# Norm sums of a two-block transformer kernel: pairs added on GpSimd, one unit back at full width, other banks, second block begun with k, q and v

## The chip, the cores and the metric

The kernel runs on one core of a Trainium2 chip. The metric is the device time of one execution in microseconds (us). The time of before is the median of three runs. Engines are named as in the profile: PE is TensorE (PEld its weight load), DVE VectorE, ACT ScalarE, POOL GpSimd, SP SyncE, which issues the DMAs of the weights.

## The reference, cut to what matters

Two transformer blocks over 512 tokens with 1024 features, all in fp32. The first holds two layers (Fox attention, then differential attention), each with a convolutional feed-forward net:

```python
def first_block(x, ...):
    for layer in range(DEPTH):                       # 2
        h = _fox_attention(...) or _diff_attention(...)
        x = _layer_norm(DN_ALPHA * x + h, ln_attn_g[layer], ln_attn_b[layer])
        f = _conv_ffn(x, ...)
        x = _layer_norm(DN_ALPHA * x + f, ln_ffn_g[layer], ln_ffn_b[layer])

def rms_norm(x, g):
    xf = x.astype(jnp.float32)
    xf = xf * lax.rsqrt(jnp.mean(xf * xf, axis=-1, keepdims=True) + EPS)
    return (xf * g.astype(jnp.float32)).astype(x.dtype)
```

The second block takes an RMS norm of that result and makes one projection out of it: keys, values and queries of a grouped-query attention with 8 query and 2 key heads, and the x, z, B, C and time-step inputs of a state-space scan (SSD) with a convolution over time. Both branches are mixed, projected, normed, added to x, and followed by a norm, a gated feed-forward net and a last norm. The change touches the eight norms. Four are layer norms, which need the mean of the values and of the squares; four are RMS norms, which need the mean of the squares alone.

## The kernel before, in words

**Data.** Activations lie feature-major: 8 blocks of 128 features by 512 tokens. Products are made to fp32 precision out of two parts of each operand: XH is the rounded activation, XL what is left of it, HI and LO the same of a weight. A weight *unit* is a slab of up to 1024 features by 256 outputs; SP loads it into RAW, ACT rounds it to HI (L1766, four instructions of 128x512), and LO = RAW - HI is made by DVE for the even quarters and by POOL for the odd ones (L2646). Each k-step of a tile is then three matmuls, HI with XH, HI with XL, LO with XH (L1441).

**Order.** `agenda()` writes one list of steps, and every engine follows that list in order, each taking the steps in which it has a part. Where work runs beside other work (attention beside the projections), `alongside()` mixes the two at a rate out of `RATES`, and `SLOW` sets how often the turning of the second block's queries gets a step. `LATE` and `STATS` hold the steps of a norm back by so many tiles.

**Halves.** A norm needs all 1024 features of a token before it can begin. `ending()` therefore runs the last units before a norm in two halves of 256 tokens: first all of their tiles for tokens 0 to 255, then for 256 to 511, with twice as many matmuls of half the width. `beginning()` does the same with the first units behind the norm, so that half 0 of the next projection can run while half 1 is normed.

**The norms.** They are called a0, f0, a1, f1 (layer norms behind attention and net of the two layers), c0 (the second block's first norm), m, p and f (RMS norms; m and p stand together, as f1 and c0 do, through `two_norms()`). YH is the residual sum that a norm works on. A1 sums its values, A2 its squares. A full-width tile (step `acc`) is squared on ACT into S and added on POOL into A2 (L2666), and its values into A1 (L2668). A tile pair of a half (step `acch`) is squared into a buffer P (L1789) and not added. The step `st0` sums over the 128 partitions on PE by matmuls with one output column each (128x1): over A2 and A1, then over every YH block and every P that was not added. For c0 and p the square of each pair (`sqp`, L1795) is followed by a step `stq` with its four one-column matmuls. Each matmul that the program orders stands in the trace as two records, so `x8` in a row of the trace is four ordered matmuls. After `st0` come `st1`, `stb` and the four pairs of `lnp` (T, XH on ACT, XL on POOL).

**Banks.** PSUM has eight banks. The norms use 6 for one half and 5 for the other; c0 and p the other way round.

**Ends of units around the change.** The attention output is four units, `ao` in layer 0 and `bo` in layer 1. Unit 0 runs at full width, 1 to 3 in halves. Units 0 and 1 of the net (`up0`, `up1`) then begin in halves. The second block begins with `ck` (keys) and `cq` 0 and 1 (queries) in halves, then `cv` (values and time steps, 160 columns) at full width, then six units `cx` whose tiles go through the convolution (cxe, cx1, cxt). The step `cacs` needs a chain on ACT with three table loads and on DVE, which starts from the last tile of `cv`.

Of the kernel before, what the change touches and what calls it, by code (L numbers as in the profile page):

```python
# [110 lines left out]
def const_arrays():  # L111
# [32 lines left out]
RATES = (0.37, 0.18, 1.15, 0.36, 1.0, 0.9, 0.9)  # L144
AHEAD = 5
SLOW = 2
# [21 lines left out]
    "acch": (("sq", 1),),  # L168
    "sqp": (("sq", 1),),
    "stq": (("ssum", 1),),  # L170
# [70 lines left out]
class Agenda:  # L241


    def __init__(self):
        self.steps, self.tiles, self.order, self.bank_of, self.free_of = [], [], [], {}, {}
        self.unit_end, self.count = {}, {}
        self.slot_of, self.slot_free = {}, {}
# [18 lines left out]
def raised(step, tiles):  # L266
# [15 lines left out]
    if k == "acc":  # L282
        _, n, j, mean = step
        adds = (1 if j == 0 else 2) if mean else (1 if j else 0)
# [24 lines left out]
def unit_sequence():  # L309
# [9 lines left out]
    out += [("ck", 0), ("cq", 0), ("cq", 1), ("cv", 0)] + [("cx", i) for i in range(6)] + [("cz", i) for i in range(4)]  # L319
# [7 lines left out]
def agenda():  # L327
# [8 lines left out]
    slots = {"S": [None] * 2, "T": [None] * 3, "P": [None] * 3}  # L336
# [16 lines left out]
    def at_slot(step, pool, q, release):  # L353

        if q is None:
            q = taken_slots[pool] % len(slots[pool])
            taken_slots[pool] += 1
        ag.slot_of[step], ag.slot_free[step] = q, slots[pool][q]
        slots[pool][q] = (release[0], release[1])
# [134 lines left out]
    def ending(n, groups, src, banks, evict, chain):  # L494
# [12 lines left out]
        for f in range(2):  # L507
            for (p, keys), bank in zip(groups, banks[f]):
# [23 lines left out]
                put("acch", n, p, f)  # L532
                at_slot(steps[-1], "P", p - 1, ("ssum", ("st0", n, f)))
# [4 lines left out]
    def beginning(units, last=False):  # L538
# [8 lines left out]
        for f in range(2):  # L547
            for q, (kind, key, widths, banks, evac) in enumerate(units):
# [13 lines left out]
                t0, rows = ts[q]  # L562
                if kind == "mm":
# [47 lines left out]
    def accumulate(n, j, mean):  # L611
        s = put("acc", n, j, mean)
        if j:
            at_slot(s, "S", None, ("ac", s))

    def chain(n, f, mean, each, begun=False):

        if not begun:
            for _ in range(LATE):
                yield  # L620
            while bank_of_norm(n, f) in norm_at:
                yield
            norm_at.add(bank_of_norm(n, f))
            s = put("st0", n, f)
            at_bank(s, bank_of_norm(n, f))
# [10 lines left out]
    def bank_of_norm(n, f):  # L636
        return 6 - (f if n not in ("c0", "p") else 1 - f)

    def normed(n, kind):
        def each(f, p):  # L640
            s = put(kind, n, f, p)
            at_slot(s, "T", None, ("xl", s))
# [6 lines left out]
    def layer_norm(n):  # L649
        return lambda f: chain(n, f, True, normed(n, "lnp"))  # L650

    def two_norms(n, n2):

        def each(f, p):
            if n == "f1":
                s = put("lnr", n, f, p)
                at_slot(s, "T", None, ("la", s))
            else:
                s = put("n1", n, f, p)
            s2 = put("sqp", n2, f, p)  # L660
            at_slot(s2, "S", None, ("ssum", ("stq", n2, f, p)))
# [2186 lines left out]
```

## Time and profile before

| | |
|---|---|
| median of 3 runs | 2492.13 us (2486.79 to 2497.16) |
| profiled execution: time, span | 2489.54 us, 2487.8 us |
| PE busy | 2332.1 us, 94% of the span |
| DVE, ACT, POOL busy | 1101.3, 1014.5, 917.1 us (44%, 41%, 37%) |
| granted TensorE clock, mean | 0.948 |

Busy time of PE is its matmul time; a granted clock of 0.5 is 1.2 GHz and 1.0 is 2.4 GHz, and a mean in between says how the stretch was shared. The chain of work that ended last runs over PE for 84% of the span, so what counts are PE's own instructions, its waits and its clock.

### The profile page before, as it was taken

Reading aid. Unit: us, or ns where it says so; the run is one execution under the profiler, and the core shown is the slowest. Engines: PE = TensorE matmul, PEld = TensorE weight load, DVE = VectorE, ACT = ScalarE, POOL = GpSimd, SP = SyncE. Lnnn points to the kernel's source line nnn. Section 1 sums busy time; section 2 is a strip of 40 time slices with the busy share of each in tenths; the row PEclk is TensorE's granted clock in tenths of the full one; section 3 lists DMA queues with packets and bytes.
Section 4 is the critical chain, followed back from the end, with each engine's and each line's share of the span. In section 5 each row is a group of like instructions: output and inputs, shape, how many; then the busy total and the mean of one; then the engine's idle time right before and its main releaser. Section 6 shows DMA issues by size and latency. Waiting matters only on the chain.

```text
span 2487.8 us, 31338 instructions
## 1 busy us (share of the span) xinstructions
PE 2332.1 (94%) x12565; PEld 1972.8 (79%) x12576; DVE 1101.3 (44%) x1826; ACT 1014.5 (41%) x2061; POOL 917.1 (37%) x718
## 2 busy tenths in 40 slices
PE   7999999999998887999999988998899999999998
PEld 6788898888887776988888887665487888888887
DVE  3545454554335664454543332545644333333322
ACT  5656354443255553344442243443244333333222
POOL 3655343344456642243344232002432332222232
PEclk9999999999999898899999886996899999999999
DMA  3111122222223210122223111000012221222221
GB/s 149 58 60 52 35 102 102 89 98 94 77 94 94 68 56 31 52 102 102 91 92 104 53 49 39 35 35 17 1 43 77 102 102 52 87 100 102 88 103 64
DMA packets 30880, 183.27 MB, mean 74 GB/s; under 512 B 3984, under 2 KB 6160, under 8 KB 12944
## 3 DMA queue, kind: packets, MB, share of 16 engines
q1 hardware_dynamic: 30736, 181.27, 20.7%
q8 instruction: 100, 1.64, 0.3%
q14 instruction: 44, 0.36, 0.0%
HBM read 174.97 MB, written 2.10 MB: 71 GB/s over the span
## 4 chain that ended last, share of the span: by engine, by line
PE 84%; DVE 5%; ACT 4%; POOL 3%; issue 2%; DMA 0%; another core or an unknown queue 0%; SPq 0%; POOLq 0%; ACTq 0%; DVEq 0%
PE PS L1441 82%; POOL LO L2646 1%; PE PS L1568 1%; PE PS L1678 1%; POOL XL L2646 1%; DVE aQS L2153 0%; ACT bP L1993 0%; DVE LO L2153 0%; ACT HI L1766 0%; DVE bQS L2153 0%; PE PS L1616 0%; POOL A_f L2666 0%; ACT bQS L1979 0%; ACT T_a L1815 0%
## 5 line engine op out<-in xcount | busy, mean ns | idle before, releaser
L2646 POOL TENSOR_TENSOR LO<-RAW,HI 128x512 fp32r<-128x512 f32 (+1 forms) x382 | 542.2, 1436 | 648.8 <-ACT HI L1766 648.6
L1441 PE MATMUL PS<-XH,HI 128*128 128x512 f32 (+2 forms) x1752 | 675.2, 385 | 40.1 <-POOL XL L2646 20.1
L1441 PE MATMUL PS<-XL,HI 128*128 128x512 f32 (+2 forms) x1752 | 657.0, 375 | 0.0
L1441 PE MATMUL PS<-XH,LO 128*128 128x512 f32 (+2 forms) x1752 | 656.7, 375 | 0.0
L1441 PEld LDWEIGHTS PS<-XH,HI 128*128 128x128 f32 (+1 forms) x1752 | 337.7, 193 | 117.4 <-issue 39.4
L2153 DVE TENSOR_TENSOR LO<-RAW,HI 128x512 fp32r<-128x512 f32 (+3 forms) x286 | 314.2, 1109 | 218.9 <-ACT HI L1766 218.9
L1766 ACT ACTIVATE HI<-RAW 128x512 fp32r<-128x512 f32 (+3 forms) x668 | 365.9, 607 | 97.4 <-DMA RAW<-wall 96.9
L1441 PEld LDWEIGHTS PS<-XH,LO 128*128 128x128 f32 (+1 forms) x1752 | 337.6, 193 | 58.5 <-issue 1.1
L1441 PEld LDWEIGHTS PS<-XL,HI 128*128 128x128 f32 (+1 forms) x1752 | 338.3, 193 | 51.8 <-issue 1.0
L1441 PE MATMUL PS<-HH,HI 128*128 128x512 f32 (+1 forms) x660 | 235.7, 357 | 3.3 <-POOL LO L2646 3.2
L1441 PE MATMUL PS<-HL,HI 128*128 128x512 f32 (+1 forms) x660 | 231.9, 351 | 0.0
L1441 PE MATMUL PS<-HH,LO 128*128 128x512 f32 (+1 forms) x660 | 231.8, 351 | 0.0
L1441 PEld LDWEIGHTS PS<-HH,HI 128*128 128x128 f32 x660 | 128.2, 194 | 21.0 <-POOL LO L2646 3.6
L1441 PEld LDWEIGHTS PS<-HL,HI 128*128 128x128 f32 x660 | 128.2, 194 | 16.9 <-issue 1.4
L1441 PEld LDWEIGHTS PS<-HH,LO 128*128 128x128 f32 x660 | 128.2, 194 | 15.4
L1441 PE MATMUL PS<-HI,XH 128*128 128x256 f32 (+1 forms) x416 | 129.4, 311 | 8.3 <-DVE aVL L2153 2.8
L2678 POOL TENSOR_TENSOR UT<-UT 128x512 f32<-128x512 f32 x44 | 56.4, 1283 | 206.2 <-ACT UT L1844 206.2
L1441 PE MATMUL PS<-LO,XH 128*128 128x256 f32 (+1 forms) x416 | 123.3, 296 | 0.0
L1441 PE MATMUL PS<-HI,XL 128*128 128x256 f32 (+1 forms) x416 | 123.3, 296 | 0.0
L1842 ACT ACTIVATE UT<-PS,SM 128x512 f32<-128x512 f32 x88 | 67.5, 771 | 126.4 <-PE PS L1441 126.4
L2251 DVE SCALAR_TENSOR_TENSOR UT<-PS,SM,UT 128x511 f32<-128x511 f32 x88 | 65.4, 744 | 93.1 <-ACT UT L1842 93.1
L2684 POOL TENSOR_SCALAR aP<-aP,aRC 128x128 f32<-128x128 f32 (+1 forms) x64 | 69.4, 1086 | 91.9 <-DVE aRC L2332 91.7
(345 smaller groups left out, 3596.0 us busy)
## 6 DMA issues: line engine op xcount, KB each, us to landing
RAW<-wall SPq DMA_DIRECT2D x138, 1024.0 KB, 4.8
RAW<-wall SPq DMA_DIRECT2D x24, 896.0 KB, 4.6
bROT<-bTQ SPq DMA_DIRECT2D x64, 64.0 KB, 2.0
RAW<-wall SPq DMA_DIRECT2D x5, 512.0 KB, 3.5
XF<-xT SPq DMA_DIRECT2D x4, 512.0 KB, 5.7
outT<-XR SPq DMA_DIRECT2D x8, 256.0 KB, 2.3
FP<-cfp SPq DMA_DIRECT2D x1, 1024.0 KB, 6.8
MKF<-cmask SPq DMA_DIRECT2D x1, 704.0 KB, 11.0
```

The lines of the kernel that those rows point to most:

```text
L1441: return e.matmul(out, a, b, start=start, stop=stop)
L1568: m = e.transpose(PS[bank][:, 128 * kb:128 * kb + 128], aP[:, 512 * (n % 4) + 128 * kb:512 * (n % 4) + 128 * kb + 128], IDN)
L1678: m = e.transpose(PS[bank][:, 128 * kb:128 * kb + 128], p[:, 128 * kb:128 * kb + 128], IDN)
L1766: act(HI[i % 3][:, c], RAW[i % 3][:, c], ACT.Copy).then_inc(SEM["hi"], 1)
L1842: act(x, PS[ag.tiles[t].bank][:, :], ACT.Identity, bias=col(f"cb{lay}", f), scale=col(f"cw{lay}2", f)).then_inc(SEM["ui"], 1)
L2153: return e.tensor_tensor(out, x, h.bitcast(F32), ALU.subtract)
L2251: e.scalar_tensor_tensor(out=x[:, 1:512], in0=ps[:, 0:511], scalar=col(f"cw{lay}1", f), in1=x[:, 1:512], op0=ALU.mult, op1=ALU.add).then_i ...
L2646: return e.tensor_tensor(out, x, h.bitcast(F32), ALU.subtract)
L2678: e.tensor_tensor(g, g, v, ALU.mult).then_inc(SEM["um"], 1)
L2684: e.tensor_scalar(p, p, aRC[:, n:n + 1], None, ALU.mult).then_inc(SEM["dg"], 1)
```

## The change

- **Sums by pairs.** A2 and A1 become 1024 wide: two tiles side by side. The squares of tiles 0 and 1 are written straight into A2, and POOL copies the values of both into A1. Every later full-width tile is added by POOL to its side, and so are now the pairs 1 and 2 of the halves (in m, and in c0 and p the pairs 1 and 2 of `sqp`). Pair 3 is still summed by PE. Buffers P and the step `stq` go; `st0` is one step for all norms.
- **Units split.** `attn_out` runs unit 1 of `ao` and `bo` at full width; halves are left for 2 and 3.
- **Banks.** Half 0 of a norm uses bank 6, half 1 bank 4 (f1, m) or 5; c0 and p use 5 and 6. The first units of the net change their banks with it.
- **Second block.** The order becomes ck, cq0, cv, cq1, of which ck, cq0 and cv begin in halves. `SLOW`, two of the `RATES`, and `LATE` for c0 and p are changed.

```diff
-RATES = (0.37, 0.18, 1.15, 0.36, 1.0, 0.9, 0.9)
+RATES = (0.37, 0.18, 1.25, 0.36, 1.6, 0.9, 0.9)
-SLOW = 2
+SLOW = 1
...
-    out += [("ck", 0), ("cq", 0), ("cq", 1), ("cv", 0)] + [("cx", i) for i in range(6)] + [("cz", i) for i in range(4)]
+    out += [("ck", 0), ("cq", 0), ("cv", 0), ("cq", 1)] + [("cx", i) for i in range(6)] + [("cz", i) for i in range(4)]
...
+    def squares(step, n, f, to_sum, add):
+
+        if add or to_sum:
+            at_slot(step, "S", ("ac", step) if add else ("ssum", ("st0", n, f)))
+        if dict(raised(step, tiles)).get("ac"):
+            add_before[step] = added.get(n)
+            added[n] = step
...
-                put("acch", n, p, f)
-                at_slot(steps[-1], "P", p - 1, ("ssum", ("st0", n, f)))
+                squares(put("acch", n, p, f), n, f, p == 3, p < 3)
...
+        for _ in range(2 if n in ("c0", "p") else LATE):
+            yield
...
     def bank_of_norm(n, f):
-        return 6 - (f if n not in ("c0", "p") else 1 - f)
+        if n in ("c0", "p"):
+            return 5 + f
+        return 6 if f == 0 else 4 if n in ("f1", "m") else 5
...
-            s2 = put("sqp", n2, f, p)
-            at_slot(s2, "S", None, ("ssum", ("stq", n2, f, p)))
-            yield
-            yield
-            s2 = put("stq", n2, f, p)
+            squares(put("sqp", n2, p, f), n2, f, p == 3, p in (1, 2))
+            yield
+            yield
...
-        ending(n, [(i, [(name, i)]) for i in (1, 2, 3)], src, [[2, 3, 4], [7, 0, 1]], residual_half(n), layer_norm(n))
+        for j, t in enumerate(lin_fm((name, 1), src)):
+            residual(n, 2 + j, t)
+        ending(n, [(i, [(name, i)]) for i in (2, 3)], src, [[4, 7], [0, 1]], residual_half(n), layer_norm(n))
...
         beginning([("mm", ("ck", 0), (128,), [0], qk_evac(4)), ("mm", ("cq", 0), (128, 128), [1, 2], qk_evac(0)),
-                   ("mm", ("cq", 1), (128, 128), [3, 4], qk_evac(2))], last=True)
-
-        def evac(c, t):
-            return ("cdt", put("cvev", c, t))
-        lin_tm(("cv", 0), "X", evac)
+                   ("mt", ("cv", 0), None, [3, 7], lambda c, t: ("cdt", put("cvev", c, t)))], last=True)
         converted[0] = True
+        for j, t in enumerate(lin_fm(("cq", 1), "X")):
+            qk_evac(2)(j, t)
...
+            elif kind in ("acch", "sqp") and step in ag.add_before:
+                n, p, f = a
...
+                e.wait_ge(*when("sq", *step))
+                if ag.add_before[step] is not None:
+                    e.wait_ge(*when("ac", *ag.add_before[step]))
+                s2, s1 = half_sums(nb["A2"], f), half_sums(nb["A1"], f)
+                e.tensor_tensor(s2, s2, by2(buf(n, "S", step)[:, :]), ALU.add).then_inc(SEM["ac"], 1)
+                if n in MEANED:
+                    e.tensor_tensor(s1, s1, pair(YH, p, f), ALU.add).then_inc(SEM["ac"], 1)
```

PE's order where a0's statistics of half 0 are made (`st0`, in the middle of the last units of `ao`; A_a_143 is A2, A_a_142 is A1, P_a are the squares of pairs that are not added), of before:

```order
L1441 MATMUL PS<-NEGC,FP 128x4
L1441 MATMUL PS<-FP,A_a_143 128x1
L1441 MATMUL PS<-FP,A_a_142 128x1
L1441 MATMUL PS<-FP,A_a_143 128x1
L1441 MATMUL PS<-FP,A_a_142 128x1
L1441 MATMUL PS<-FP,YH 128x1 x4
L1441 MATMUL PS<-FP,P_a_150 128x1 x4
L1441 MATMUL PS<-FP,YH 128x1 x4
L1441 MATMUL PS<-FP,P_a_151 128x1 x4
L1441 MATMUL PS<-FP,YH 128x1 x4
L1441 MATMUL PS<-FP,P_a_149 128x1 x4
```

The same place of the changed kernel:

```order
L1447 MATMUL PS<-NEGC,FP 128x4
L1447 MATMUL PS<-FP,A_a_143 128x1
L1447 MATMUL PS<-FP,A_a_142 128x1
L1447 MATMUL PS<-FP,A_a_143 128x1
L1447 MATMUL PS<-FP,A_a_142 128x1
L1447 MATMUL PS<-FP,A_a_143 128x1
L1447 MATMUL PS<-FP,A_a_142 128x1
L1447 MATMUL PS<-FP,A_a_143 128x1
L1447 MATMUL PS<-FP,A_a_142 128x1
L1447 MATMUL PS<-FP,YH 128x1 x4
L1447 MATMUL PS<-FP,S_a_145 128x1 x4
```

28 ordered one-column matmuls became 16; the 128x4 one ahead of them stays.

POOL's order from the first tile of `ao` to the odd quarters of LO_61, the first unit of the net (LO_59 and LO_60 are those of the last two `ao` units; XL is the norm's own), of before:

```order
L2661 COPY A_a_142<-YH 128x512
L2666 TENSOR_TENSOR A_a_143<-A_a_143,S_a_144 128x512
L2668 TENSOR_TENSOR A_a_142<-A_a_142,YH 128x512
L2646 TENSOR_TENSOR LO_59<-RAW_56,HI_62 128x512 x2
L2646 TENSOR_TENSOR LO_60<-RAW_57,HI_63 128x512 x2
L2646 TENSOR_TENSOR XL<-T_a_146,XH 128x2x256
L2646 TENSOR_TENSOR XL<-T_a_147,XH 128x2x256
L2646 TENSOR_TENSOR XL<-T_a_148,XH 128x2x256
L2646 TENSOR_TENSOR XL<-T_a_146,XH 128x2x256
L2646 TENSOR_TENSOR LO_61<-RAW_58,HI_64 128x512 x2
```

And of the changed kernel, up to the first XL:

```order
L2640 TENSOR_TENSOR LO_59<-RAW_56,HI_62 128x512 x2
L2661 TENSOR_TENSOR A_a_143<-A_a_143,S_a_144 128x512
L2663 TENSOR_TENSOR A_a_142<-A_a_142,YH 128x512
L2661 TENSOR_TENSOR A_a_143<-A_a_143,S_a_145 128x512
L2663 TENSOR_TENSOR A_a_142<-A_a_142,YH 128x512
L2640 TENSOR_TENSOR LO_60<-RAW_57,HI_63 128x512
L2671 TENSOR_TENSOR A_a_143<-A_a_143,S_a_144 128x2x256
L2673 TENSOR_TENSOR A_a_142<-A_a_142,YH 128x2x256
L2640 TENSOR_TENSOR LO_60<-RAW_57,HI_63 128x512
L2671 TENSOR_TENSOR A_a_143<-A_a_143,S_a_144 128x2x256
L2673 TENSOR_TENSOR A_a_142<-A_a_142,YH 128x2x256
L2640 TENSOR_TENSOR XL<-T_a_146,XH 128x2x256
```

Six more additions stand there, and LO_60, the last `ao` unit's, lies between them, the second odd quarter behind the additions of half 0's pair 2.

ACT's order at the end of `ao`, where the squares of the last pairs and the rounding of the net's first weights (HI_64) lie, of before:

```order
L1819 ACTIVATE XH<-T_a_146 128x2x256
L1789 ACTIVATE P_a_151<-YH 128x512
L1766 ACTIVATE HI_64<-RAW_58 128x512 x4
L1789 ACTIVATE P_a_149<-YH 128x512
L1766 ACTIVATE HI_62<-RAW_56 128x512 x2
```

And of the changed kernel:

```order
L1813 ACTIVATE XH<-T_a_146 128x2x256
L1789 ACTIVATE S_a_145<-YH 128x512
L1762 ACTIVATE HI_64<-RAW_58 128x512 x4
L1762 ACTIVATE HI_62<-RAW_56 128x512 x2
```

In the changed kernel the square ahead of HI_64 is that of the last pair (3) of half 1, and no longer that of pair 2.

## Rows read from the trace of the kernel before

A line of a timeline gives the start in us, the duration in us from first to last instruction of the group, the engine, the line of the kernel, and how many records it holds; in brackets stands the idle time before it and what ended it.

**Rows 1.** The page: busy time of each engine.

```profile
PE 2332.1 (94%) x12565; PEld 1972.8 (79%) x12576; DVE 1101.3 (44%) x1826; ACT 1014.5 (41%) x2061; POOL 917.1 (37%) x718
```

**Rows 2.** Busy time by stretch: us, engines' busy (count), granted clock, DMA share, GB/s.

```profile
983.00:1062.00 79.00, 76.06 (x575) 74.85 (x576) 35.16 (x51) 30.13 (x58) 28.81 (x21) 0.91 0.15 54
1376.00:1476.00 100.00, 85.46 (x574) 83.33 (x573) 35.08 (x61) 32.95 (x65) 29.07 (x22) 0.81 0.12 41
1476.00:1552.00 76.00, 65.67 (x381) 57.85 (x381) 22.11 (x43) 31.41 (x59) 21.58 (x17) 0.73 0.17 58
1701.00:1726.00 25.00, 19.43 (x75) 13.86 (x74) 12.87 (x20) 10.03 (x19) 5.13 (x3) 0.51 0.01 5
2044.00:2120.00 76.00, 70.42 (x561) 69.38 (x560) 27.38 (x46) 28.75 (x53) 21.13 (x15) 0.96 0.16 56
```

**Rows 3.** Waits of PE over the whole span: us, times, longest.

```profile
PE PS L1441 <- ACT S_m L1795: 2.1, 3, 0.8
...
PE PS L1441 <- ACT cPT L2071: 1.6, 2, 0.8
```

**Rows 4.** Waits of PE from 1405 to 1552 us: us, times, longest.

```profile
PE PS L1441 <- POOL XL L2646: 9.4, 4, 3.3
PE PS L1441 <- DVE cADT L2496: 6.1, 1, 6.1
PE PS L1441 <- ACT S_f L1795: 3.5, 2, 1.7
PE PS L1441 <- ACT FP L2076: 2.6, 1, 2.6
PE PS L1441 <- DVE LO L2153: 1.6, 1, 1.6
```

**Rows 5.** Timeline of PE, a0's statistics of half 0: start, us, work.

```profile
292.06 0.28 PE L1441 MATMUL PS<-aOH,LO 128*128 128x256 f32 x1
292.18 0.28 PE L1441 MATMUL PS<-NEGC,FP 128*128 128x4 f32 x2
292.31 1.03 PE L1441 MATMUL PS<-FP,A_a 128*128 128x1 f32 x8
293.21 1.03 PE L1441 MATMUL PS<-FP,YH 128*128 128x1 f32 x8
...
301.53 0.56 PE L1441 MATMUL PS<-aOH,HI 128*128 128x256 f32 x1
```

**Rows 6.** Busy time by stretch around both halves' statistics of a0.

```profile
291.00:302.00 11.00, 11.00 (x72) 11.00 (x71) 0.26 (x2) 1.36 (x2) 0.00 (x0) 0.70 0.01 1
302.00:306.00 4.00, 4.00 (x22) 4.00 (x22) 0.64 (x4) 0.30 (x1) 0.00 (x0) 0.55 0.01 2
320.00:330.00 10.00, 10.00 (x75) 10.00 (x73) 1.94 (x4) 1.76 (x4) 1.82 (x2) 0.80 0.21 87
330.00:334.00 4.00, 4.00 (x24) 4.00 (x24) 1.18 (x4) 1.86 (x4) 1.28 (x1) 0.64 0.00 0
```

**Rows 7.** Timeline of POOL in the last units of ao.

```profile
272.69 1.30 POOL L2666 TENSOR_TENSOR A_a<-A_a,S_a 128x512 f32<-128x512 f32 x1 [1.40 <-ACT S_a L1783]
273.95 1.74 POOL L2668 TENSOR_TENSOR A_a<-A_a,YH 128x512 f32<-128x512 f32 x1
275.65 3.42 POOL L2646 TENSOR_TENSOR LO<-RAW,HI 128x512 fp32r<-128x512 f32 x2
```

**Rows 8.** Timeline of DVE, then ACT, at the end of ao.

```profile
288.78 0.69 DVE L2191 SCALAR_TENSOR_TENSOR YL<-XL,PS 128x512 f32<-128x512 f32 x1 [4.35 <-PE PS L1441]
...
316.35 2.18 ACT L1766 ACTIVATE HI<-RAW 128x512 fp32r<-128x512 f32 x4
```

**Rows 9.** Timeline of ACT before cacs.

```profile
1535.03 1.28 ACT L2047 ACT_TABLE_LOAD   x1
```

**Rows 10.** Timeline of PE, then DVE, behind the last cx unit.

```profile
1725.77 0.98 PE L1441 MATMUL PS<-cBC 128*128 128x128 f32 x3 [3.34 <-DVE cBC L2542]
...
1703.80 0.74 DVE L2530 SCALAR_TENSOR_TENSOR cCVT<-FP,SM,cCVT 128x510 f32<-128x510 f32 x1
```

More of the change, by code:

```diff
@@ L607, in lin_tm, with accumulate, chain @@
             freed[tiles[t].bank] = evac(c, t)
[L611 to L619, printed above, removed]
-                yield
-            while bank_of_norm(n, f) in norm_at:
-                yield
-            norm_at.add(bank_of_norm(n, f))
-            s = put("st0", n, f)
-            at_bank(s, bank_of_norm(n, f))
+    def accumulate(n, j):
+        squares(put("acc", n, j), n, None, False, j > 1)
+    def chain(n, f, each):
+        for _ in range(2 if n in ("c0", "p") else LATE):
+            yield
+        while bank_of_norm(n, f) in norm_at:
+            yield
+        norm_at.add(bank_of_norm(n, f))
+        s = put("st0", n, f)
+        at_bank(s, bank_of_norm(n, f))
+        ag.last_add[n, f] = added.get(n)
         put("st1", n, f)
@@ L802, in ffn_up @@
         count = 3 if lay == "2" else 2
-        beginning([("mm", ("up" + lay, j), (128, 128), ([2, 3], [4, 7], [0, 1])[j], up_evac(lay, j)) for j in range(count)],
+        beginning([("mm", ("up" + lay, j), (128, 128), ([2, 3], [7, 0], [1, 4])[j], up_evac(lay, j)) for j in range(count)],
                   last=count == 3)
-        lin["banks"] = [2, 3, 4, 7, 0, 1] if count == 3 else [0, 1, 2, 3, 4, 7]
+        lin["banks"] = [2, 3, 7, 0, 1, 4] if count == 3 else [1, 4, 2, 3, 7, 0]
         lin["n"] = 0
@@ L1047, in xconv, with x_evac @@
                 turns.append(j)
+        def x_evac(jj, t):
+            freed[tiles[t].bank] = ("cxe", put("cxe", jj, t))
+            chores.append(xconv(jj))
         def xbc(i):
@@ L1353, in NORM_BANK @@
     def NORM_BANK(n, f):
[L1354 removed]
+        return PS[ag.bank_of["st0", n, f]]
     def sums_made(n, f):
[L1357 removed]
+        return when("ssum", "st0", n, f)
     def buf(n, pool, step):
@@ L1506, in tensor @@
-                for p in pairs_of[n]:
-                    if mean:
-                        e.wait_ge(*y_half(n, p, f))
-                        for q in range(2):
-                            for c in range(2):
-                                y = blk(YH, 2 * p + q)[:, 256 * f + 128 * c:256 * f + 128 * c + 128]
-                                mm(PS[bank][:, 2 + c:3 + c], y, MEAN[:, 0:1], False, False)
-                    e.wait_ge(*when("sq", "acch", n, p, f))
+                e.wait_ge(*(when("sq", "sqp", n, 0, f) if second else when("sq", "acc", n, 1)))
@@ new lines, in tensor @@
+                if ag.last_add[n, f] is not None:
+                    e.wait_ge(*when("ac", *ag.last_add[n, f]))
+                for q in range(2):
+                    for c in range(2):
+                        t = slice(512 * q + 256 * f + 128 * c, 512 * q + 256 * f + 128 * c + 128)
+                        mm(PS[bank][:, c:c + 1], nb["A2"][:, t], MEAN[:, 0:1], False, False)
+                        if mean:
+                            mm(PS[bank][:, 2 + c:3 + c], nb["A1"][:, t], MEAN[:, 0:1], False, False)
@@ L1526, in tensor @@
+                last = ("sqp" if second else "acch", n, 3, f)
+                e.wait_ge(*when("sq", *last))
                 for q in range(2):
                     for c in range(2):
-                        y = sq[:, 256 * q + 128 * c:256 * q + 128 * c + 128]
-                        done = mm(ps[:, c:c + 1], y, MEAN[:, 0:1], False, p == 3 and q == 1 and c == 1)
+                        y = buf(n, "S", last)[:, 256 * q + 128 * c:256 * q + 128 * c + 128]
+                        done = mm(PS[bank][:, c:c + 1], y, MEAN[:, 0:1], False, q == 1 and c == 1)
```

140 lines of the change are left out of this document (59 added, 81 removed).

## The prediction

> **What bounds the kernel now.** I read the page first: PE is busy for 2332.1 of 2487.8 us, while DVE, ACT and POOL are busy for less than half of the span [rows 1]. So a change can save time in three ways only: fewer PE instructions, fewer PE waits, or more of the span at the full TensorE clock. I then read the busy time by stretch. The dense stretches run at clock 1.00; the stretches that hold a norm do not. Around a1 PE is busy for 76.06 of 79 us, at 0.91. From 1376 to 1476 (f1, c0, first unit of block two) it is 85.46 of 100 us at 0.81, the next 76 us have 65.67 at 0.73, the 25 us behind the last cx unit 19.43 at 0.51, and around m and p it is 70.42 of 76 us at 0.96 [rows 2]. What the clock costs is (1 - clock) times busy: 6.8, 16.2, 17.7, 9.5 and 2.8 us. The waits came third: S_m and cPT are short [rows 3], and those of block two's start are 9.4 + 6.1 + 3.5 + 2.6 + 1.6 = 23.2 us [rows 4].
>
> The timeline at a0 shows why. Before the statistics a matmul of 256 columns starts every 0.12 us. Then eight one-column records take 0.90 us from start to start, 0.112 each, and the ordered 28 + 1 matmuls, 58 records, last from 292.18 to 301.53: 9.35 us where 58 x 0.112 = 6.5 would do [rows 5]. The rest is the clock: 0.70 from 291 to 302 and 0.55 for 4 us more; around half 1 it is 0.80 and 0.64 [rows 6]. That makes 3.3 + 1.8 + 2.0 + 1.4 = 8.5 us lost at a0.
>
> **The change, part by part** (minus is a gain).
>
> *Statistics of a0 and a1.* Each half falls from 58 to 34 records: 24 x 0.112 x 2 = -5.4 us a norm [rows 5]. The shorter stretch of one-column work should also leave the clock alone for longer: 58 records lose 2.9 us of the 9.35 to it, and 34 records last 3.8 in all. I take 5.1 of the 8.5 back at a0 and half of the 6.8 at a1: -10.5 and -8.8. The bounds of the clock part are nothing and the whole, 15.3 for both.
>
> *What POOL does in its place.* POOL gets six more additions and a copy here, the additions at 1.30 us (S) and 1.74 us (YH) [rows 7]. POOL is idle for most of this stretch, so they cost nothing as such; but LO of the last `ao` unit now stands between them. Its second odd quarter comes after two additions (3.0 us) which wait for pair 2 of half 0. From the pair's last matmul run YL and YH (0.69 each), the square (0.6, as an HI of that shape), the additions and the LO itself (half of 3.42): some 6.6 us with the first quarter's slack [rows 7, 8]; PE needs it some 2.1 us on, three quarters of the way through a tile of 24 matmuls of 0.12. So PE waits some 4.4 us; about 1.2 of such waits stood here before: +3.2 a norm. If DVE's and ACT's work delays the additions further it is 6; if PE's other tile covers it, 0.
>
> *Weights of the net's first unit.* ACT's square of the last pair now stands ahead of HI_64, so the rounding starts only when PE has no `ao` matmul left. From the last matmul: YL 0.69, YH 0.69, square 0.6, two HI at 0.55 (four in 2.18), then POOL's two odd quarters, 3.42 us for both [rows 7, 8]: the last is ready some 6.5 to 7 us behind that matmul, and of the first tile's own work (24 matmuls of 0.12, 2.9 us) 2.1 lie ahead of it. PE waits 4 to 5: I take +5.0 a norm. Before, the rounding lay beside 48 matmuls and the wait was nil. The idle time should bring the clock down once more, +1.5 a norm (7 us at a mean of 0.8).
> Sum for a0 and a1: -19.3 + 6.4 + 10.0 + 3.0 = +0.1. The full-width unit has as many columns as its halves, so I count nothing for it. Bounds: -15 and +10.
>
> *f0, f1, f.* Most of their tiles were added in full already; now two sides have to be summed: 34 records a half where there were 26 for f0 and f1, 18 for 14 for f. 8 x 0.112 x 2 = +1.8 for f0, with the clock +2.2, and +0.5 for f.
>
> *f1, c0 and the start of block two.* c0's squares were 34 records a half in four steps, now 18 in one: -3.6; with f1's +1.8, -1.8. The waits for S_f (3.5) go. In their place c0's statistics wait for two POOL additions and XL of the first pair, much as now: of the 12.9 us at ck and cq (XL 9.4, S_f 3.5) about 11.6 stay, for XL comes behind the additions. cq1's odd LO now stands behind the turning of the earlier queries on POOL (two adds of 1.3): its wait goes from 1.6 to about 6.7. The end of `cv` is further ahead, yet `cacs` still waits for its chain with three table loads of 1.28 us [rows 4, 9]: FP and cADT 8.7 become about 11, as cq1 alone lies between. Waits: 23.2 become 29.3, +6. The clock is the gain: 16.2 + 17.7 = 34 us are lost from 1376 to 1552 [rows 2]. `cv`, with its short 160-column matmuls, gets the 512-wide tiles of cq1 behind it, and the one-column pieces lie together. I take 12 of 34, about a third, for rows 6 have the clock back some 4 us behind such a piece; bounds 0 and 24. Sum -7.8, bounds +4 and -21.
>
> *Attention of block two.* Between the last cx matmul and cBC, 24.7 us, lies attention at clock 0.51 with a wait of 3.34 at its end, while the convolution is done by DVE in steps of 0.74 [rows 2, 10]. With the rates raised, attention is over sooner and only the chain of the last two tiles stays: 8 DVE steps x 0.74 + two copies, activations and one product, some 11.8 us. That saves 12.9. The PE work that leaves is 19.43 x 0.51 less 1.4 for cBC, 8.5 us, and comes back ahead of it at full clock. Net -4.4; bounds 0 and -11 (if it fills waits).
>
> *m and p.* 12 and 16 records a half fewer, at 0.112: 2 x (1.3 + 1.8) = -6.3. The S_m waits, 2.1, go [rows 3], and 1.7 of the 2.8 us of clock. LO of co2 and co3 comes behind additions, +3.8, and the first XL pair by 1.3. Sum -5.0; bounds -9 (the waits on LO and XL don't come) and +3 (they are twice as long, and the clock gives nothing).
>
> The sum: 0.1 + 2.2 + 0.5 - 7.8 - 4.4 - 5.0 = -14.4. The profiled execution took 2489.5, which gives 2475.1; the median of the runs is 2.6 us above it, so 2477.7, and I put 2477.
>
> **A rule beside it.** The Trainium skill, "TensorE: Matmul & The Clock Gate", section "Why this matters for your kernels", warns of idle gaps between bursts of matmuls, since the engine falls back to half clock after them. The trace agrees in so far as the stretches with the most idle time have the lowest clock [rows 2]. By that rule the new waits at HI_64 and LO would cost their length twice over; that is rival A. The "GPSIMD Engine Reference", section 4.1, has additions of two inputs about twice as slow on GpSimd as on VectorE; here 1.30 and 1.74 stand against 0.69 on DVE, and PE pays for that only where LO or XL stands behind them.
>
> **Rivals.**
> A, no change, 2480 to 2504, most likely 2497: the waits for HI_64 and LO at a0 and a1 (16.4 us together) are each followed by half clock for as long again, and block two's start gives back 6 of its 12 us of clock. That is 16 less 3 already counted, and 6, on a sum of -14: +5, 2494 for the profiled execution and 2497 for the median; with the LO waits partly hidden it is 2490. For it: PE is busy for 76.06 of 79 us there [rows 2], so nothing else can take the delay. Against: in rows 6 the clock is back some 4 us behind the statistics.
>
> B, slower, 2510: attention too dense. 32 rounds (8 heads, 4 blocks) are now laid among fewer projection tiles. Where a round's softmax is not done, PE waits for cPT, 0.8 each time, which now happens twice [rows 3]. If all 32 waited 0.8 us, 25.6 in all, and the gaps cost as much clock again as the tail loses now, 9.5 [rows 2], that is +35 on a sum of -14: 2512. It takes the side of slower from +27 on, that is, when some 24 rounds wait so. For it: a round's softmax runs over ACT and DVE, which hold the convolution too, and SLOW 1 brings the turning of the queries forward beside it. Against: two waits in 32 now.
>
> C, much faster, 2463: HI_64's rounding is hidden after all, because half 1's last `ao` tiles are evicted before PE has finished its others, and the clock stays up at a0 and a1 (-10 and -4).
>
> D, the shorter sums save nothing, because the one-column matmuls were hidden: excluded, since PE is busy without a gap through them [rows 6].
>
> **How the numbers follow.** The forecast has 0.42, A 0.24, B 0.14, C 0.20. This kernel's measurement can tell 0.5% (12.5 us, so below 2479.7 or above 2504.6). The forecast's own range is 2467 to 2487, and about two thirds of it lie on the faster side: 0.28. With C's 0.20 and 0.01 of A faster is 0.49; slower is nearly all of B and a little of A, 0.15; same the rest, 0.36. The range reaches from 2458 (C and less) to 2502 (A's upper end): outside lie most of B (0.12) and the lowest few hundredths of C.
>
> **What would show it.** In the new trace a0's statistics should last 3.8 to 5 us a half; PE should wait 4 to 5 us for LO with HI_64 at the first net unit of layers 0 and 1, and 3 to 5 for the last `ao` LO; no wait for S_f or S_m may be left; 1376 to 1552 should have a mean clock of 0.85 or so; between the last cx matmul and cBC there should be about 12 us with hardly any PE work. I am wrong if the HI_64 wait is under 2 us (C), if the clock behind it stays at half for over 6 us (A), or if waits for cPT and its like pass 16 us in sum (B).

## The result

The changed kernel takes 2508.55 us (median of 5 runs, 2501.33 to 2510.79) where the kernel before takes 2491.76 (5 runs, 2482.42 to 2497.16): a ratio of 1.007, 95% interval 1.0042 to 1.0099. It is 0.7% slower, clear of the noise. I had forecast 2477 and a range up to 2502. Its profiled execution took 2501.33 us, the fastest of its five; so the traces show 11.7 us of loss in the span, and the medians 17. That execution also had the highest mean clock of the five (0.946; the others 0.942 to 0.944).

The page of the changed kernel, busy time of each engine, against [rows 1]:

```profile
span 2499.5 us, 30824 instructions
...
PE 2316.9 (93%) x12288; PEld 1952.7 (78%) x12288; DVE 1106.5 (44%) x1826; ACT 1013.3 (41%) x2065; POOL 940.9 (38%) x740
```

PE has 277 records fewer and is busy for 15 us less; yet the span is longer. Its waits over the whole span:

```profile
PE PS L1447 <- POOL XL L2640: 20.9, 14, 4.0
PE PS L1447 <- POOL LO L2640: 18.8, 10, 3.3
PE PS L1447 <- issue: 14.8, 6, 5.4
PE PS L1447 <- DVE cBC L2536: 10.6, 1, 10.6
...
PE PS L1447 <- DVE cADT L2490: 7.4, 1, 7.4
```

LO has gone up from 5.6 us, and "issue" from 6.5, with single waits of 3.3 and 5.4 us that the kernel before doesn't have. The timeline of PE around a0 shows two of them (a1 has the same pair):

```profile
288.93 0.28 PE L1447 MATMUL PS<-aOH,LO 128*128 128x256 f32 x1
292.51 0.58 PE L1447 MATMUL PS<-aOH,HI 128*128 128x256 f32 x1 [3.30 <-POOL LO L2640]
...
302.61 1.93 PE L1447 MATMUL PS<-FP,A_a 128*128 128x1 f32 x16
304.40 1.03 PE L1447 MATMUL PS<-FP,YH 128*128 128x1 f32 x8
305.29 1.72 PE L1447 MATMUL PS<-FP,S_a 128*128 128x1 f32 x8
306.87 0.56 PE L1447 MATMUL PS<-aOH,HI 128*128 128x256 f32 x1
...
323.69 0.56 PE L1447 MATMUL PS<-XH,HI 128*128 128x256 f32 x1 [5.41 <-issue]
```

The statistics of half 0 now take 4.4 us where [rows 5] have 9.35. POOL shows why the first gap is there: the two additions of pair 2 stand between the odd quarters of the last unit's LO.

```profile
285.72 1.73 POOL L2640 TENSOR_TENSOR LO<-RAW,HI 128x512 fp32r<-128x512 f32 x1
288.75 1.27 POOL L2671 TENSOR_TENSOR A_a<-A_a,S_a 128x512 f32<-128x512 f32 x1 [1.29 <-ACT S_a L1789]
289.98 1.26 POOL L2673 TENSOR_TENSOR A_a<-A_a,YH 128x512 f32<-128x512 f32 x1
291.19 1.26 POOL L2640 TENSOR_TENSOR LO<-RAW,HI 128x512 fp32r<-128x512 f32 x1
```

ACT shows the second: the last pair's square, and the rounding of the net's first weights right behind it, while PE had its last `ao` matmul at 318.0.

```profile
321.71 0.63 ACT L1789 ACTIVATE S_a<-YH 128x512 f32<-128x512 f32 x1 [0.28 <-DVE YH L2189]
322.25 3.21 ACT L1762 ACTIVATE HI<-RAW 128x512 fp32r<-128x512 f32 x6
```

And the busy time by stretch gives what came with them. Of PE's columns the first is busy time; the number behind POOL's is the clock. First come the whole stages of a0 and a1, then the four stretches at a0 that hold half clock: behind the first gap, from the statistics on, behind the second gap, and from the statistics of half 1 on:

```profile
268.00:352.00 84.00, 73.22 (x462) 69.95 (x462) 35.88 (x50) 30.79 (x57) 35.58 (x28) 0.84 0.14 51
990.00:1076.00 86.00, 75.15 (x464) 71.46 (x465) 35.59 (x51) 29.38 (x56) 35.95 (x28) 0.82 0.14 50
...
292.00:299.00 7.00, 6.49 (x32) 6.49 (x33) 0.00 (x0) 0.00 (x0) 0.46 (x1) 0.53 0.00 0
304.00:313.00 9.00, 9.00 (x53) 9.00 (x54) 2.03 (x6) 0.75 (x2) 0.00 (x0) 0.62 0.10 21
323.00:330.00 7.00, 6.31 (x33) 6.34 (x33) 3.63 (x3) 2.56 (x6) 4.66 (x3) 0.55 0.01 2
332.00:341.00 9.00, 9.00 (x53) 9.00 (x53) 1.68 (x6) 1.86 (x4) 1.28 (x1) 0.62 0.00 0
```

Stage by stage, from marks that both traces have (a wait or the first matmul of a kind), in us:

| stage | before | after | difference | forecast |
|---|---|---|---|---|
| a0: last wait for aOL to the last wait for XL at up1 | 78.3 | 84.0 | +5.7 | } +0.1 |
| a1: last wait for bOL to the last wait for XL at up1 | 76.7 | 85.6 | +8.9 | } |
| between the two (f0 in it) | 636.8 | 638.0 | +1.3 | +2.2 |
| from there to cacs (f1, c0, start of block two) | 482.3 | 468.7 | -13.6 | -7.8 |
| cacs to cBC (cx units, attention) | 183.6 | 191.1 | +7.5 | -4.4 |
| cBC to the first `co` matmul | 308.1 | 305.1 | -3.0 | 0 |
| `co`, m, p, to the wait for LO at 2145 / 2155 | 111.2 | 114.2 | +3.0 | -5.0 |
| to the end (f) | 342.7 | 344.8 | +2.1 | +0.5 |

The rest, -0.2, lies ahead of a0. By the program's order 27 projection matmuls that stood ahead of cacs stand behind it now, 6.1 us of 512 columns at full clock; with them put back the fourth line is -7.5 and the fifth +1.4.

Every row is one execution. In the ten traces here that share the changed block two (the changed kernel and nine of the experiments below), cacs to cBC took 188.2 to 196.4 us and cBC to `co` 305.0 to 308.1; the kernel before and the three that share its block two have 183.6 and 308.1. So the -3.0 is not the change's (most of the ten don't have it), and the +1.4 could as well be -1.5 or +6.7.

### The profile page after: what moved, and what is told of

Same layout as the page of the kernel before. It is cut to its first block, busy times and chain, and to the rows that moved or that the text cites. A ratio compares the mean times of both kernels' runs of the same rounds, so it can differ in the third digit from the quotient of the medians.

```text
span 2499.5 us, 30824 instructions
## 1 busy us (share of the span) xinstructions
PE 2316.9 (93%) x12288; PEld 1952.7 (78%) x12288; DVE 1106.5 (44%) x1826; ACT 1013.3 (41%) x2065; POOL 940.9 (38%) x740
## 4 chain that ended last, share of the span: by engine, by line
PE 82%; DVE 6%; ACT 5%; POOL 3%; issue 2%; DMA 0%; SPq 0%; POOLq 0%; ACTq 0%; DVEq 0%
PE PS L1447 81%; POOL LO L2640 1%; PE PS L1564 1%; POOL XL L2640 1%; PE PS L1674 1%; DVE aQS L2147 0%; ACT HI L1762 0%; DVE cCVT L2524 0%; DVE XR L2236 0%; ACT bP L1987 0%; ACT T_a L1809 0%; DVE YH L2231 0%; DVE bQS L2147 0%; PE PS L1612 0%; DVE LO L2147 0%
## 5 line engine op out<-in xcount | busy, mean ns | idle before, releaser
L2147 DVE TENSOR_TENSOR LO<-RAW,HI 128x512 fp32r<-128x512 f32 (+2 forms) x286 | 318.1, 1122 | 225.3 <-ACT HI L1762 225.0
L1762 ACT ACTIVATE HI<-RAW 128x512 fp32r<-128x512 f32 (+2 forms) x668 | 365.7, 607 | 97.0 <-DMA RAW<-wall 96.6
```

Source lines behind the costliest of these rows:

```text
L1762: act(HI[i % 3][:, c], RAW[i % 3][:, c], ACT.Copy).then_inc(SEM["hi"], 1)
L2147: return e.tensor_tensor(out, x, h.bitcast(F32), ALU.subtract)
```

## The experiments

Theory G: the gaps at a0 and a1, each with a stretch of half clock behind it, are the loss. Rival R: it lies in block two (idle tail, rates). All stages "a0" below are measured as in the table (78.3 before, 84.0 changed), in the one profiled execution of each kernel; ratios are against the kernel before, on the same chips.

### HI_64 earlier (x1_cut)

```diff
                     if f and key == first:
-                        hold[0] = HOLD
+                        hold[0] = HOLD if len(groups) != 2 else 1
```

> The changed kernel with one edit: at the end of ao and bo the rounding of the net's first weights (HI_64) is released at the start of half 1's last unit, and so three of its four instructions stand ahead of the last pair's square, as in the kernel before. Theory G (the new idle gaps at a0 and a1, each followed by about 6 us at half clock, made the change slower): the wait of 5.4 us at up0 and up1 falls under 1 us and the half-clock stretch behind it goes: 2 x (5 + 3) = 16 us less than the changed kernel, profile about 2485. Rival R (the loss lies in block two, where attention ends early and PE idles for 13 us, or in the rates): a0 and a1 give back the idle time but something else waits instead; under 5 us in all.

Measured: 2506.76 us, ratio 1.0067 (1.0037 to 1.0098), stage a0 84.0. No gain. The gap at up0 fell only from 5.4 to 3.8 us, now on POOL's last LO quarter, and half clock lasted 16 us behind it:

```profile
325.00:341.00 16.00, 15.50 (x72) 15.51 (x73) 2.50 (x6) 3.51 (x8) 5.88 (x5) 0.50 0.00 1
```

The statistics of half 1 fell into that stretch (at 329.5), and the two half-clock stretches of the changed kernel grew into one. So a gap that is made smaller, not removed, may give nothing.

### LO ahead of the additions (x2_lo), and both (x3_both)

```diff
+                if not f and due[0] is not None:
+                    for _ in due[0]:
+                        pass
                 freed[bank] = evict(p, t, f)
                 squares(put("acch", n, p, f), n, f, p == 3, p < 3)
```

> The changed kernel with one edit: in half 0 of an ending what is left of the next unit's HI and LO is issued ahead of the pair's eviction, so that POOL makes LO before it adds the pair. Theory G: the LO waits of 3.3 us at a0 and a1 and of 2.2 + 1.8 us at m fall to about 1 each and the half clock behind them (6 us long, 3 us of time each) goes: 2 x (2.2 + 3) + 2 x 1 + 1 = about 13 us less than the changed kernel, profile about 2488. Rival R: the eviction comes later behind the additional LO on DVE and POOL, and the same wait moves to the statistics: no gain.

Measured: 2488.36 us, ratio 1.0003 (0.9981 to 1.0025): 20 us less than the changed kernel, and as fast as before. The waits for LO at a0, a1 and m are gone; stage a0 76.2, a1 80.5, m and p 109.8 (from 114.2). The span fell by 18.3, of which these three give 17.3. The gap of 5.4 us at up0 is still there.

> Both edits of the two kernels before on the changed kernel. Theory G: the gains add up, 16 + 13 = 29 us less than the changed kernel: profile about 2472, 0.7% faster than the kernel before. If idle gaps and one-column statistics share one half-clock stretch each, the clock's part is less and it is about 2480. Rival R: about the time of the changed kernel.

Measured: 2481.42 us, ratio 0.9979 (0.996 to 0.9998). At a0 76.8, no better than LO alone: 3.8 us of gap at up0 and again one long stretch behind it, as the windows show:

```profile
317.00:335.00 18.00, 17.04 (x82) 17.04 (x83) 2.52 (x6) 3.97 (x9) 6.36 (x5) 0.53 0.00 1
```

### Three units in halves again (x4_halves)

```diff
-        for j, t in enumerate(lin_fm((name, 1), src)):
-            residual(n, 2 + j, t)
-        ending(n, [(i, [(name, i)]) for i in (2, 3)], src, [[4, 7], [0, 1]], residual_half(n), layer_norm(n))
+        ending(n, [(i, [(name, i)]) for i in (1, 2, 3)], src, [[2, 3, 4], [7, 0, 1]], residual_half(n), layer_norm(n))
```

> The changed kernel with unit 1 of ao and bo in halves again (three units in halves, as before the change); the sums by pairs, the banks and block two stay changed. If the full-width unit is what put the rounding of HI_64 behind the last square, the wait of 5.4 us goes by this alone: about 2 x (5.4 + 3) = 16 us less, but the additions of one more pair a half stand ahead of LO on POOL, and two LO waits of 2 to 3 us in place of one: some 4 to 8 back, profile 2490 to 2493. If the additions on POOL are the cause instead, it is no faster than the changed kernel.

Measured: 2507.19 us, ratio 1.0073 (1.0046 to 1.0099), stage a0 83.4. The wait of 5.4 us at up0 goes indeed (0.8 and 1.1 us are left), but LO comes behind the additions twice, 4.7 and 3.8 us. In all, PE waits for LO in that stage, where the kernel before has 1.1 us:

```profile
PE PS L1445 <- POOL LO L2638: 9.6, 3, 4.7
```

So the change is as slow without its full-width unit.

### The full-width unit alone (y1_full)

The kernel before with only the diff of x4_halves in reverse.

> The kernel before the change with one part of it alone: unit 1 of ao and bo at full width, units 2 and 3 in halves. The sums stay on PE as before. Then HI_64 stands behind the last square without any addition on POOL between: a wait of 5.4 us with 3 us of clock at up0 and up1 is +17, less 16 one-column records a norm and a half (the pair 1 is now in A2): -3.6 x 2; profile about 2498. If the wait needs POOL's additions to come about, it is 2485.

Measured: 2493.51 us, ratio 1.0012 (0.9991 to 1.0032), stage a0 78.1. The gap of 5.4 us at up0 does come by this edit alone. POOL has four additions a norm more by it, those of the unit's two full-width tiles, but none of the half pairs' (its records go from 718 to 726), and no wait for LO comes of them (0.5 us). At a0 the gap is about paid for by the sums that the edit shortens (58 records a half become 42), at a1 it is not (79.7 us from 76.7). I had +10 for this wait at both norms; the medians are 7 us apart (2486.74 before), and the interval of the ratio includes no difference at all.

```profile
PE PS L1443 <- issue: 5.4, 1, 5.4
```

### HI_64 from the start of half 1 (x5_early)

With LO first, as x2_lo.

```diff
         for f in range(2):
+            if f and len(groups) == 2:
+                hold[0] = 1
```

> The changed kernel with LO ahead of the pair's additions (as the second kernel above) and, in place of the late release, the rounding of HI_64 released at the start of half 1 of ao and bo: now all four instructions stand ahead of the last square. If the wait of 3.8 us at up0 and up1 that was left comes from the last quarter alone, it goes (under 1 us), and with it the half-clock stretch of 16 us that ran from it through half 1's statistics: 2 x (3.8 + 4) = about 15 us less than with the late release, profile 2466 to 2474. If that stretch comes from the one-column statistics and not from the gap, only the 3.8 us go: about 2474 to 2482.

Measured: 2480.36 us, ratio 0.9967 (0.9948 to 0.9986). In the profiled execution PE waits at up0 for 0.8 us only, stage a0 is 70.0 and a1 68.5, and half clock comes only with the statistics:

```profile
296.00:304.00 8.00, 8.00 (x47) 8.00 (x47) 0.65 (x4) 1.69 (x4) 0.72 (x1) 0.61 0.00 0
320.00:325.00 5.00, 5.00 (x31) 5.00 (x31) 1.34 (x5) 1.86 (x4) 1.29 (x1) 0.67 0.00 0
```

The medians of x3_both and x5_early differ by 1 us, though, and their profiled executions by 17: the first was among x3's slowest (2490.78), the second among x5's fastest (2474.08). How much of the stage's gain is there in every execution of this kernel stays open.

### Statistics in pieces (x6_split, z1_late, u1_mean)

On x5_early, `st0` is cut into four steps: the sums over the first side of A2 and A1, over their second side, over YH and over the last square, with one tile step (six projection matmuls) between two.

```diff
-        for _ in range(2 if n in ("c0", "p") else LATE):
+        for _ in range(2 if n in ("c0", "p") else 1 if n in MEANED else LATE - 1):
             yield
...
-        s = put("st0", n, f)
-        at_bank(s, bank_of_norm(n, f))
         ag.last_add[n, f] = added.get(n)
+        for q in range(3 if n in MEANED else 1):
+            s = put("sta", n, f, q)
+            if q == 0:
+                at_bank(s, bank_of_norm(n, f))
+            yield
+        ag.bank_of[put("st0", n, f)] = bank_of_norm(n, f)
...
```

> The kernel before (LO first, HI_64 from the start of half 1), and the statistics of every norm in two to four pieces of at most 9 ordered one-column matmuls, with six projection matmuls between two pieces. Theory: it is the unbroken stretch of 18 to 34 one-column records that brings half clock for some 6 us; in pieces it does not come, as c0 and p showed before the change: 13 statistics with 2 to 3 us each, about 25 us less at most, I say 15. Rival: the clock falls all the same, and the longer way to the statistics puts 1 to 2 us of waits on XL at each norm: 5 to 10 us more.

Measured: 2470.6 us, ratio 0.9928 (0.9902 to 0.9953), 10 us less than x5_early, stage a0 64.0. The whole stage, and the stretches of the two statistics, run at full clock with as many one-column records as in x5_early (the five traces with this order at a0, of x6_split, z1_late, z2_tail, u1_mean and u2_rates, all have 64.0):

```profile
268.00:332.50 64.50, 61.89 (x463) 58.61 (x463) 34.35 (x51) 30.70 (x57) 36.06 (x28) 1.00 0.19 66
294.00:302.00 8.00, 8.00 (x71) 8.00 (x71) 2.27 (x7) 3.76 (x7) 1.27 (x1) 1.00 0.01 3
311.00:319.00 8.00, 8.00 (x72) 8.00 (x71) 3.89 (x9) 4.94 (x11) 5.71 (x4) 1.00 0.29 120
```

Around m and p it lost: 120.4 us where x5_early has 112.2. PE's waits there are

```profile
PE PS L1456 <- POOL XL L2654: 7.9, 3, 3.1
PE PS L1456 <- POOL A_m L2685: 3.8, 1, 3.8
```

The wait for POOL's additions (A_m) is no longer than that of x5_early, 4.0 us; XL was 4.4 there, and the mean clock of the stage is 0.89 where x5_early has 0.94.

> The kernel with statistics in pieces (LO first, HI_64 from the start of half 1), with one number changed: in m and f the first piece comes one tile step later, as late as the single step of the changed kernel. In the version before it PE waited 3.8 us for POOL's additions A_m and 3.1 + 2.6 + 2.3 us for XL around m and p, and the clock was down for 12 us of busy time. If the early piece is what brought that, the wait for A_m falls to about 1 us and m and p give back 6 to 8 us: median about 2463. If the pieces themselves delay the norm there, it stays at 2470.

Measured: 2470.71 us, ratio 0.9926 (0.9903 to 0.9949); the stage at m and p took 120.8. The early first piece was not the reason.

u1_mean puts the extra `yield` behind `if n in MEANED`, so that c0, m, p and f have one step again.

> The version with pieces, LO first and HI_64 early, with pieces for the four layer norms alone; c0, m, p and f have their statistics in one step. Around m and p the pieces made the stage 5 to 7 us longer than without them (117 to 119 against 112 us). If that is the pieces, this kernel is 5 to 7 us faster: median about 2464.

Measured: 2463.26 us, ratio 0.989 (0.9866 to 0.9913), the stage at m and p 112.8, so it was the pieces that had cost there. This version is 1.1% faster than the kernel before, and 45 us faster than the changed one (ratios 0.989 and 1.007).

### Pieces without the rest (v1_after_split, w1_before_split, w2_all_but_sums)

v1_after_split is z1_late without the edits of x2_lo and x5_early.

> The changed kernel with the statistics in pieces and nothing else (HI_64 and LO stay where the change put them). By the stage times the waits of 3.3 and 5.4 us at a0 and a1 stay, and with them two stretches of half clock at each; the two behind the statistics go: 2 x 6 us, and 6 at f0 and f1: about 15 less than the changed kernel, median 2492. If the pieces do as much as in the version with LO and HI_64 moved (-10), 2497. If the idle gaps keep the clock down by themselves and swallow it all, 2506.

Measured: 2509.63 us, ratio 1.008 (1.0058 to 1.0101), stage a0 83.7: no gain at all there, and m and p take 120.8 for 114.2, as with the pieces above. The second gap is followed by 20 us of half clock:

```profile
321.00:341.00 20.00, 19.37 (x93) 19.41 (x94) 4.90 (x8) 4.35 (x10) 5.92 (x4) 0.51 0.00 1
```

w1_before_split cuts the statistics of the kernel before, as they are, into pieces of four ordered matmuls.

> The kernel before the change, with its own statistics in pieces of four ordered one-column matmuls (up to seven pieces for a0 and a1, six projection matmuls between two). All else is as before the change. If it is the unbroken stretch that brings half clock, the 8.5 us at a0, 6.8 at a1, 3.3 at f0 and some 3 at each of f1 and m come back: about 22 us, median 2465. If the shorter sums on PE are needed for it, the many pieces keep the clock down or bring XL waits: under 8 us.

Measured: 2492.82 us, ratio 1.0028 (1.0006 to 1.0049). Half 0's seven pieces ran at full clock; half 1's began 1 us ahead of a wait of 1.1 us for LO, and 21 us of half clock followed:

```profile
288.00:312.00 24.00, 24.00 (x206) 23.89 (x205) 10.01 (x19) 10.17 (x19) 4.19 (x3) 1.00 0.25 89
316.00:337.00 21.00, 21.00 (x103) 21.00 (x102) 3.46 (x8) 4.14 (x9) 4.17 (x3) 0.51 0.01 1
```

w2_all_but_sums adds to w1_before_split the full-width unit, LO first and HI_64 from the start of half 1.

> The kernel before the change, block two and banks as before, with unit 1 of ao and bo at full width, LO ahead of the pair, HI_64 from the start of half 1, and the statistics in pieces; the pairs are summed on PE. It differs at a0 and a1 from the version with pieces only in that PE sums pair 2 itself: 8 more one-column matmuls a half. If POOL's sums are what the gain at a0 and a1 needs, this stage stays above 70 us where the pieces version has 64; if the order of LO and HI and the pieces do it, the stage takes 66 and the median is about 2470.

Measured: 2481.15 us, ratio 0.9974 (0.9958 to 0.999), stage a0 67.4. So of the 14 us that x6_split gained at a0, POOL's sums (with x6_split's other banks) give 3.4 at most; the order of LO and HI with the pieces gives the rest. Elsewhere (m and p 116.8, with pieces) it lacks what u1_mean has.

### Block two (y2_rates, t1_order, z2_tail, u2_rates)

y2_rates is the changed kernel with RATES and SLOW as before; t1_order the kernel before with order, RATES and SLOW as changed; z2_tail is z1_late with RATES 1.15 in place of 1.25; u2_rates is u1_mean with RATES and SLOW as before.

> The changed kernel with the numbers of block two undone: SLOW 2 and RATES 1.15 and 1.0, while the order ck, cq0, cv, cq1 stays. If the higher rates are worth something, it is slower than the changed kernel: attention lies again behind the last cx unit at half clock, 24 us in place of 20 (wait for cBC 3 in place of 13 us), but the stretch before it is shorter by about the same work. By my sum the rates are worth 4.4 us: profile about 2505. If their gain is lost in the stretch before, it is 2500 or less.

Measured: 2503.16 us, ratio 1.0066 (1.0049 to 1.0084), cacs to cBC 194.4, inside the 188.2 to 196.4 of the kernels with the changed rates. The ratio is that of the changed kernel: the rates are worth nothing.

> The kernel before the change with the third part of it alone: block two begun with ck, cq0, cv, then cq1, and the changed RATES and SLOW. By the stage times of the changed kernel this part is worth 6 us from the end of the last net of block one to cBC, together with c0's sums; if all of it is the order and the rates, this kernel is 5 to 8 us faster than the one before it: median about 2481. If it is the sums of c0 that gave it, it is as fast as before or slower, 2487 to 2492.

Measured: 2488.37 us, ratio 0.9995 (0.9981 to 1.0009). Block two's part alone is worth nothing: it takes 9.7 us less up to cacs and 7.4 more from there to cBC.

> The same kernel with one rate more undone: RATES 1.15 in place of 1.25 during the cx units, so that some attention is left for the 13 us in which PE now waits for the convolution behind the last cx unit (2.8 + 10.6 us for cBC). If work moved into that gap is free, the gap falls to 5 us or less and the time by the same 5 to 8 us of full-clock work less what half clock takes of it: 3 to 4 us less. If the idle engine was no loss, because the convolution sets the end there anyway: within 1 us.

Measured: 2481.37 us, ratio 0.9973 (0.9955 to 0.999), 11 us slower than z1_late; cacs to cBC 204.2 in place of 188.7, with a wait of 14.8 us for cBC and not of less. The work didn't go into the gap, and what it cost is half clock. The stretch in z1_late, then in z2_tail:

```profile
1511.00:1699.70 188.70, 164.59 (x794) 113.40 (x795) 94.96 (x167) 79.17 (x163) 24.24 (x17) 0.93 0.10 34
1508.70:1713.00 204.30, 176.88 (x795) 121.45 (x795) 96.23 (x167) 79.26 (x163) 23.66 (x17) 0.85 0.09 31
```

Why this one rate lowers the clock stays open.

> The kernel before (pieces for the layer norms alone) with the numbers of block two undone: SLOW 2, RATES 1.15 and 1.0. With the changed numbers attention is over 12 us ahead of cBC and PE idles for it; a first try with 1.15 beside 1.6 made it 11 us slower. If the rates are worth what the stage times of the changed kernel showed, it is 3 us slower, 2467; if the idle tail is the loss, it is 3 to 5 us faster.

Measured: 2464.29 us, ratio 0.9892 (0.9869 to 0.9914). Against u1_mean no difference. PE's waits around cacs and up to cBC are other ones: the changed kernel has 10.6 and 2.8 us for cBC, 7.4 for cADT and 5.2 for FP, and u2_rates has

```profile
PE PS L1457 <- ACT FP L2085: 8.7, 5, 4.0
...
PE PS L1457 <- DVE cADT L2505: 3.7, 1, 3.7
...
PE PS L1457 <- DVE cBC L2551: 1.0, 1, 1.0
```

## Why the prediction was wrong

**The step that failed** is the clock at a0 and a1: "I take 5.1 of the 8.5 back at a0 and half of the 6.8 at a1", and "The idle time should bring the clock down once more, +1.5 a norm". The other terms of that sum held: statistics of 4.4 us in half 0; 3.8 us of LO waits a norm where 1.1 stood before (forecast 4.4 for 1.2); 5.4 for HI_64 (5.0). But (1 - clock) times busy is 11.7 us over the stage of a0 and 13.5 at a1 (rows above), where 8.5 and 6.8 were before (the four stretches at a0 by themselves give 12.7; the clock of a long stretch is rounded more coarsely). I had -3.6 and -1.9 for it, and it was +3 and +7. Two parts of the step failed.

First, each gap brought its own stretch of half clock, some 7 us long. By the rows above that costs (1 - 0.53) x 6.49 = 3.1 us behind the LO gap, for which I had put nothing, and 2.8 behind HI_64, for which I had 1.5. Second, the shorter statistics gave hardly any clock back. In half 0 of a0, 34 records cost 0.38 x 9.00 = 3.4 us where the 58 cost 5.1 [rows 6]; in half 1 they cost 3.4 as before. That is 1.7 us and not 5.1. At a1 both halves lost 3.4 before and lose it now. Rival A had the gaps' mechanism (half clock "for as long again"); I gave it 0.24, and its end (2504) lay short of the result because the stages below didn't give what I had counted.

**m and p** had the same fault, and with it 8 us of the miss. The S_m waits went and LO waits of 2.2 + 1.8 us came, as forecast; waits for A_m (1.0) and YH (1.8) came beside them, and the clock cost 6 us where it had cost 3, not 1.7 less: +3.0 in all, not -5.0. Before, then changed:

```profile
2034.00:2145.00 111.00, 103.21 (x780) 99.40 (x779) 40.54 (x67) 44.17 (x79) 33.68 (x25) 0.97 0.22 77
2040.50:2154.70 114.20, 100.73 (x726) 96.55 (x724) 44.60 (x67) 44.42 (x81) 42.72 (x32) 0.94 0.22 74
```

x2_lo gave 4.4 us of it back.

**cacs to cBC** was to save 4.4 by moving attention out of the tail. The tail itself did as I said: from the place where the forecast's 24.7 us begin (the last products for cBC) it is 11.7 us for 11.8, nearly empty. The work moved ahead of it cost more there than its full-clock price, and +1.4 remains in this execution. t1_order says that the whole part is worth nothing, y2_rates and u2_rates that the rates are. That attention displaces other work at its own price, and that the convolution sets the end, fit this; they were not tried by themselves.

**What was right**: f0 (+1.3 for +2.2), no wait for S_m, and PE's wait for LO with HI_64. Rival B (attention too dense) did not happen: cPT waits 0.5 us. For f the sum is 4 records x 0.112 x 2 = 0.9, not the 0.5 of the forecast.

**What was right by luck**: the start up to cacs, -7.5 for -7.8. The waits rose by 1.4 us there and not by 6 (24.6 from 1421 to 1568, for 23.2 in [rows 4]), and the clock gave 5 and not 12. From the first half clock behind f1's statistics to cacs, before and changed, it cost 0.25 x 117.72 = 29.4 and 0.24 x 101.75 = 24.4 us:

```profile
1401.20:1542.19 140.99, 117.72 (x729) 110.34 (x728) 43.21 (x83) 56.92 (x108) 39.62 (x31) 0.75 0.16 54
1418.20:1544.32 126.12, 101.75 (x628) 94.14 (x626) 45.10 (x82) 53.68 (x104) 43.47 (x34) 0.76 0.15 52
```

Two errors of 5 to 7 us cancelled. So the forecast counted on more clock than came in each of the stages a0, a1, start of block two, and m and p.

**The cause.** x2_lo puts POOL's LO ahead of its additions and brings back all 17 us; x1_cut, which moves HI_64 alone, brings none; x4_halves, which keeps the additions and drops the full-width unit, is as slow as the changed kernel; y1_full and t1_order, the other two parts alone, are as fast as before. So the loss is that of POOL's additions standing ahead of LO; x2_lo has all of them still, so it is their place and not their number. R is refuted. Theory G holds for the LO gaps, at m as well, which it had left out. For the gap at HI_64 it holds only with LO first: x5_early (0.9967) is then some 9 us below x2_lo (1.0003), though their intervals overlap slightly. On the changed kernel the smaller gap of x1_cut gave nothing, and removing it entirely without LO first was not tried. The 5 us by which the medians differ more than the profiled executions go with the clock (0.946 against 0.942 to 0.944), in which stage is not on record.

## What to carry to other kernels

Work that is moved to an idle engine is free only if nothing that the bound engine waits for stands behind it in that engine's order: look for the next LO, XL or square behind each new instruction, and put that first. A short gap costs its length and the half clock behind it, here 3 to 10 us more, and a smaller gap can cost as much as a larger. So remove all the gaps and thin stretches of one place together, and judge them together: of the 45 us between the changed kernel and u1_mean, LO first gave 17 by itself, while the late release of HI_64 (x1_cut) and the pieces (v1_after_split) each gave nothing alone. Once the gaps are gone, try the sums in pieces between dense work, one norm at a time: they gained at a0 and a1 and lost at m and p.

## What the runs showed of the hardware

Thirty-four one-column matmul records in a row, with PE never idle, brought the granted clock from 1.00 to 0.50 in the changed kernel as 58 did before, but not alike each time. In half 0 of a0 the 34 cost 3.4 us of clock in the changed kernel and 1.7 in x2_lo (0.81 over the 9 us from 295). The same block in half 0 of a1 in x5_early cost none:

```profile
1009.00:1017.00 8.00, 8.00 (x72) 8.00 (x71) 2.39 (x8) 1.04 (x5) 1.27 (x1) 1.00 0.13 19
```

Thirty-four in pieces of 8 to 10, with six 256-column matmuls between two, left it at 1.00 (x6_split), and so did 58 in seven pieces (w1_before_split, 288 to 312 us). The same pieces around or behind a gap of PE of 1.1 (w1_before_split) or 5.4 us (v1_after_split) came with 20 us at 0.50, and one block of 34 behind a gap of 3.8 with 16 (x1_cut, x3_both), where dense matmuls alone behind a gap had it back in 6 to 7 us.

The executions of one kernel differ by 15 us (x3_both, 2476 to 2491, 12 runs) and 26 (before, 2475 to 2501, 25 runs) with the same program. The mean granted clock of each execution is on record and goes with it: in those 25 it runs from 0.954 at 2475.3 us to 0.941 at 2501.5, about 21 us for 0.01. So what differs is how long PE runs at half clock; in which stages is not on record, since only one execution of each kernel was traced.
